# First attention of a two-block layer on one core: a head's first two groups of transposes leave the middle of the projection and join the short matmuls at the head's border

## What is computed

```python
q = rms_norm(q, q_norm_g) * (HEAD_DIM ** -0.5)
...
sc = jnp.einsum('brnikgh,brnjkh->brnkgij', ql, kb, preferred_element_type=jnp.float32)
...
sc = jnp.where(valid[:, None, None], sc + bias, -jnp.inf)
m = jnp.max(sc, axis=-1, keepdims=True)
p = jnp.exp(sc - m)
l = jnp.sum(p, axis=-1, keepdims=True)
o = jnp.einsum('brnkgij,brnjkh->brnikgh', p / l, vb.astype(jnp.float32))
...
alpha = jax.nn.softmax(jnp.stack(lses), axis=0)
o = jnp.sum(alpha[..., None] * jnp.stack(outs), axis=0).astype(x.dtype)
y = o.reshape(bsz, s, B_WIDTH) * jax.nn.silu(z)
```

## Time and profile before

| | us |
|---|---|
| median of 3 runs (lowest, highest) | 1373.73 (1373.12, 1374.71) |
| the profiled execution, its own time | 1375.31 |
| its span in the profile | 1373.5 |
| TensorE busy with matmuls (PE) | 1364.8 (99%) |
| TensorE's weight loads (PEld, beside PE) | 1169.5 (85%) |
| VectorE (DVE) busy | 1058.7 (77%) |
| ScalarE (ACT) busy | 718.5 (52%) |
| GpSimd (POOL) busy | 51.0 (4%) |

### The profile page before, as it was taken

One profiled execution on the slowest core, in us unless ns is written; L12 is line 12 of the kernel. 1 busy time (PEld: TensorE's weight loads), 2 busy tenths in 40 slices (PEclk: granted clock), 3 DMA queues, 4 the chain that ended last, 5 costly groups with the idle time before them and its releaser, 6 DMA issues.

```text
span 1373.5 us, 21419 instructions
## 1 busy us (share of the span) xinstructions
PE 1364.8 (99%) x7923; PEld 1169.5 (85%) x7923; DVE 1058.7 (77%) x1787; ACT 718.5 (52%) x1260; POOL 51.0 (4%) x55
## 2 busy tenths in 40 slices
PE   8999999999999999999999999999999999999999
PEld 6998888888889878888888787787688998998997
DVE  6976777777899788888888877778867965983883
ACT  4744333223357566666663566766646642662561
POOL 0000000000100000000001100000030000000000
PEclk9999999999999999999999999999999999999999
DMA  9994445457743211112212231111131232333232
GB/s 378 382 354 188 177 181 183 183 201 279 293 155 108 93 62 63 62 62 74 78 62 66 88 124 63 64 60 62 48 107 64 91 123 67 119 123 124 69 116 92
DMA packets 35350, 181.51 MB, mean 132 GB/s; under 512 B 4153, under 2 KB 4921, under 8 KB 20930
## 3 DMA queue, kind: packets, MB, share of 16 engines
q1 hardware_dynamic: 34050, 177.95, 35.7%
q10 hardware_dynamic: 1216, 2.44, 0.6%
HBM read 177.74 MB, written 2.11 MB: 131 GB/s over the span
## 4 chain that ended last, share of the span: by engine, by line
PE 97%; DVE 1%; ACT 1%; issue 0%; DMA 0%; DVEq 0%; ACTq 0%
PE acc L2121 72%; PE turn L2708 7%; PE ada L2121 4%; PE turn L2121 3%; PE norm L2121 3%; PE ada L2708 2%; PE acc L2708 2%; PE norm L2708 2%; PE turn L2565 1%; PE turn L2422 1%; DVE y_half L1209 0%; DVE w_lo L1217 0%; DVE wv_lo L1217 0%; ACT sq L697 0%; DVE k_t L1209 0%
## 5 line engine op out<-in xcount | busy, mean ns | idle before, releaser
L2121 PE MATMUL acc<-h_hi,w_hi 128*128 128x512 f32 x696 | 277.8, 399 | 0.0
L2121 PE MATMUL acc<-h_hi,w_lo 128*128 128x512 f32 x696 | 272.0, 391 | 0.0
L2121 PE MATMUL acc<-h_lo,w_hi 128*128 128x512 f32 x696 | 271.3, 390 | 0.0
L1217 DVE TENSOR_TENSOR w_lo<-w_raw,w_hi 128x2048 fp32r<-128x2048 f32 x58 | 136.4, 2352 | 27.7 <-ACT w_hi L680 27.7
L2121 PEld LDWEIGHTS acc<-h_hi,w_lo 128*128 128x128 f32 x696 | 130.6, 188 | 28.4
L2121 PEld LDWEIGHTS acc<-h_hi,w_hi 128*128 128x128 f32 x696 | 131.0, 188 | 27.1 <-issue 1.2
L2121 PEld LDWEIGHTS acc<-h_lo,w_hi 128*128 128x128 f32 x696 | 130.9, 188 | 25.6
L680 ACT ACTIVATE w_hi<-w_raw 128x2048 fp32r<-128x2048 f32 x60 | 114.3, 1906 | 29.4 <-PE acc L2121 28.6
L1209 DVE SCALAR_TENSOR_TENSOR x<-acc,mods,x 128x512 f32<-128x512 f32 x48 | 38.7, 813 | 68.6 <-PE acc L2121 68.6
L2121 PE MATMUL acc<-wv_hi,h_hi 128*128 128x256 f32 x320 | 90.5, 284 | 0.0
L2121 PE MATMUL acc<-wv_lo,h_hi 128*128 128x256 f32 x320 | 89.1, 279 | 0.0
(11 more groups left out here) (372 smaller groups left out, 3489.8 us busy)
## 6 DMA issues: line engine op xcount, KB each, us to landing
w_raw<-in_weights SPq DMA_DIRECT2D x102, 1024.0 KB, 4.9
ada_v<-in_ada SPq DMA_DIRECT2D x32, 512.0 KB, 6.3
ada_raw<-in_ada SPq DMA_DIRECT2D x32, 512.0 KB, 5.6
ada_out<-in_ada SPq DMA_DIRECT2D x32, 512.0 KB, 6.5
ada_up<-in_ada_first SPq DMA_DIRECT2D x8, 1024.0 KB, 16.3
w_raw<-in_weights SPq DMA_DIRECT2D x4, 768.0 KB, 4.3
x<-in_x SPq DMA_DIRECT2D x2, 1024.0 KB, 6.1
w_first<-in_weights SPq DMA_DIRECT2D x4, 512.0 KB, 13.3
```

The costliest lines, as they stand in the source:

```text
L1217: nc.vector.tensor_tensor(lo[:, 0:used], w_raw[par][:, 0:used], f32(hi[:, 0:used]), ALU.subtract).then_inc(lo_done, 1)
L2121: return nc.tensor.matmul(out, lhsT, rhs, start=start, stop=stop)
```

## The change

On TensorE, `turn(0)` and `turn(1)` no longer stand ahead of piece 3 in a projecting round. They open the next round instead, and the border gets a new order: transposes 0, 1 (of the head before), scores 0, 1, transposes 2, 3, values 0, 1, scores 2, 3, values 2, 3. In round 8, which doesn't project, transposes 0 and 1 of its own head stay about where they were. On ScalarE, `rstd_start(k + 2)` moves ahead of the copies of transposes 0 and 1, and the two passes of `z_start` ahead of the copies of 2 and 3. No instruction is added or removed, and SyncE's, GpSimd's and VectorE's queues are as they were.

```diff
--- before.py
+++ after.py
@@ -882,11 +882,12 @@
                     act.wait_ge(sum_done, k + mi)
                     square(G[mi % 2], sq_hi_q, sq[0])
 
+                if attend:
+                    z_start()
                 if mho is not None:
                     for c in (2, 3):
                         turn_copy(m - 1, c)
                 if attend:
-                    z_start()
                     exps(0)
                     exps(1)
                 if project:
@@ -908,11 +909,11 @@
                     rstd_start(k + 1, NB[:, :], P)
                     to_hi(u0 + 1, 0)
                     squares(2)
+                if project:
+                    rstd_start(k + 2, NB[:, :], P)
                 if attend:
                     for c in range(2 if project else 4):
                         turn_copy(m, c)
-                if project:
-                    rstd_start(k + 2, NB[:, :], P)
 
             def out_round(n, p, mho):
 
@@ -2414,23 +2415,25 @@
                     pe.wait_ge(apart_done, m + 1)
                     mm(T1[:, 0:64], spread, row_apart[:, :, :].rearrange("p c n -> p (c n)"), True, True).then_inc(spread_done, 1)
 
-                def turn(c):
-                    pe.wait_ge(p_ready, 4 * m + c + 1)
-                    if c >= 2:
-                        pe.wait_ge(pt_act, 4 * m + c - 1)
-                    for b, (tile, lo) in enumerate(TURNS[c]):
-                        turned = nc.tensor.transpose((T0, T1)[c % 2][:, P * b:P * b + P], s_b[tile][:, lo:lo + P], ident)
-                    turned.then_inc(turn_done, 1)
-
+                if prior:
+                    turn(m - 1, 0)
+                    turn(m - 1, 1)
                 if attend:
                     scores(0)
                     scores(1)
                 if prior:
-                    for c in (2, 3):
-                        values(m - 1, p, c)
+                    turn(m - 1, 2)
+                    turn(m - 1, 3)
+                    if not (isinstance(n, int) and n == 2):
+                        pe.wait_ge(head_out, m - 1)
+                    values(m - 1, p, 0)
+                    values(m - 1, p, 1)
                 if attend and prior:
                     scores(2)
                     scores(3)
+                if prior:
+                    values(m - 1, p, 2)
+                    values(m - 1, p, 3)
                 if project:
                     piece(0)
                 else:
@@ -2442,23 +2445,27 @@
                     piece(2)
                 else:
                     early_output(1, (0, 4, 1, 5), 6)
-                if attend:
-                    turn(0)
-                    turn(1)
                 if project:
                     piece(3)
                 else:
+                    turn(m, 0)
+                    turn(m, 1)
                     early_output(1, (2, 6), 6)
-                if attend:
-                    if prior:
-                        pe.wait_ge(head_out, m)
+                    pe.wait_ge(head_out, m)
                     values(m, q, 0)
                     values(m, q, 1)
-                    turn(2)
-                    turn(3)
-                if not project:
+                    turn(m, 2)
+                    turn(m, 3)
                     early_output(1, (3,), 7)
                     early_output(0, (3,), 7)
+
+            def turn(m, c):
+                pe.wait_ge(p_ready, 4 * m + c + 1)
+                if c >= 2:
+                    pe.wait_ge(pt_act, 4 * m + c - 1)
+                for b, (tile, lo) in enumerate(TURNS[c]):
+                    turned = nc.tensor.transpose((T0, T1)[c % 2][:, P * b:P * b + P], s_b[tile][:, lo:lo + P], ident)
+                turned.then_inc(turn_done, 1)
 
             def values(m, q, c):
```

## The result

| | kernel before | changed kernel |
|---|---|---|
| median of 6 runs each, same chip | 1373.14 us (1372.72 to 1374.71) | 1379.95 us (1378.16 to 1382.16) |
| ratio after to before | | 1.0049 [1.0038, 1.006] |
| profiled execution: time, span, granted clock | 1375.31, 1373.5, 1.00 | 1378.78, 1377.0, 1.00 |

The change makes the kernel 6.8 us slower (5.2 to 8.2 us by the interval). The forecast was 1378.9 us and slower, with a range of 1376.0 to 1381.2; the result lies in it.

What follows compares the result with a forecast made beforehand. TensorE, busy 1364.8 of 1373.5 us, was taken as the bound. Rounds 2 to 7 pay 4.20, round 1 1.08, round 8 gives back 0.11: 5.2 us slower, median 1378.9 us, whole range 1376.0 to 1381.2.

Steps and rivals of the forecast that it cites:

- first wait: TensorE waits for sq_lo_q at the sums inside piece 3, rounds 2 to 7: 0.31 plus 0.09, 0.40 us each.
- second wait: TensorE waits for VectorE's q_n at a border's first scores: 0.23 plus 0.09, 0.32 us in each of seven borders.
- moved group: Seven transposes moved from ahead of piece 3 to the border: 0.78 us saved, 0.76 paid, -0.02 a round; round 1 saves nothing.
- The first meeting: Sums inside piece 3 need sq_lo_q: TensorE there after 5.70 us, the other engines' chain allows 6.01.
- sums to sums: Time from norm<-sq_lo_q of piece 1 to norm<-sq_hi_q of piece 2: 6.48 us before, forecast 6.01.
- The second meeting: First scores need VectorE's last q_n pass: possible 3.96 us after piece 2's norm<-sq_lo_q, TensorE there at 3.73.
- 0.09 behind each wait: After a TensorE wait the next matmul stands 0.33 us behind instead of 0.24; charged at all 13 waits.
- rival (c): Further waits at scores 3, values 2 or the loop's register waits: 1.4 us more and up, 1380.3 to 1383; chance 0.10.
- 1.4 us kept for scores 3: Bound for a possible TensorE wait on VectorE's logits 1 at scores 3: 0.2 us in each of seven borders, none charged.
- (a): Rival: only one of the two waits comes, 1376.5 us with the second alone, 1376.7 with the first; chance 0.09.
- (b): Rival: not slower, ScalarE's passes run sooner and both chains end before TensorE arrives; 1374.3 us; chance 0.09.
- (d): Rival: TensorE's clock falls to 1.2 GHz in borders of 75 short matmuls; about 1437 us; chance 0.01.

Runs made afterwards that it cites:

- experiment 1: Changed kernel with ScalarE's squares of piece 2 ahead of its 1.90 us weight pass in rounds with attention; 1376.36 us, ratio 1.0022 to the kernel before.
- experiment 5: Kernel of experiment 1 with the sums of piece 2 ten matmuls into piece 3, not twelve; 1373.92 us, ratio 1.0009 to the kernel before.
- experiment 3: Kernel before with only the sums in piece 3 three matmuls earlier, transposes in their old place; 1376.12 us, ratio 1.0016.
- experiment 7: Changed kernel with the rounds loop written out on TensorE, ScalarE and VectorE, every wait against a constant; 1378.60 us, ratio 1.0043 to the kernel before.
- experiment 10: Changed kernel with ScalarE's z_start passes behind the copies of transposes 2 and 3 again; 1379.4 us in one run.
- experiment 8: The kernel before, unchanged, profiled a second time; 1373.42 us, span 1371.6.
- experiment 6: Kernel of experiment 5 with VectorE freeing piece 3's accumulator in round 1 ahead of the reciprocal's second half and z's gate; 1374.48 us, ratio 1.0009.
- experiment 4: Changed kernel with ScalarE's copies of transposes 0 and 1 ahead of rstd_start(k + 2) again; 1421.08 us in one run.

## Why the prediction was right

The runs split the 6.00 us. Taking the first wait away gives 226.96 - 224.18 = 2.78, the second too 224.18 - 221.70 = 2.48, and 0.74 is left (experiments 1 and 5).

| term | predicted | measured |
|---|---|---|
| first wait, rounds 2 to 7 | 6 x 0.40 = 2.40 | 2.78 |
| second wait, borders 1 to 7 | 7 x 0.32 = 2.24 | 2.48 |
| moved group: 6 x -0.02, 0.76 in border 1, -0.11 in round 8 | 0.53 | 0.74 |
| sum in the rounds | 5.17 | 6.00 |

- **Moving the group.** With no waits, rounds are as long as before to within the 0.03 us that they scatter by; over distances 2 to 6 of experiment 5 that is 0.03 more in all, where five times -0.02 would be -0.10. So the move is free, as forecast, and its small gain is not seen. In round 1's border the group was to cost 0.76; the first distance of experiment 5 has 0.81.
- **The first meeting.** Shown. TensorE by itself would be there after 5.70 us (5.69 in experiment 1), sums to sums is the forecast 6.01 in the rounds outside the loop, and experiment 3 shows the same end with the transposes in their old place.
- **The second meeting.** Shown: 3.96 us in every border that is outside the loop. The 0.09 behind each wait held too, 0.33 against 0.24; that the late weight load makes it is argued, and no run tested it. The Trainium skill (TensorE: Matmul & The Clock Gate, Step-by-step: what each phase is for) says that weight loads are pulled ahead of matmuls in flight. The step speaks of no load behind an unmet wait, and at such a place the trace shows none pulled ahead: the load at 578.71 begins with its matmul, and the 1.2 us less that the prediction worked out from the rule did not come.
- **The mis-sized term.** The forecast took both waits as long in the loop as in rounds 0 and 1, and priced the alternative only under rival (c). In the loop the first takes 0.07 us more in rounds 3 to 6 and the second 0.085 in four borders: 0.62 us of the 0.83 that are missing, and experiment 7 gives back 0.61. With it the two waits come to 4.64 + 0.62 = 5.26, which is 2.78 + 2.48 as measured. The other 0.21 lie in the third row: by the distances of experiment 5 round 1 pays 0.81 for 0.76, distances 2 to 6 together 0.03 for -0.10, and the last -0.10 for -0.13. They have no cause shown.
- **Round 1** pays 1.14 (1.08), and its idle place is as described. **Round 8's** 0.11 came, 0.34 to 0.24, but not for the reason given. The prediction had TensorE come later against the others; experiment 10 leaves TensorE as late and has the wait back. The gain belongs to `z_start`'s new place, so that term was right by luck.
- **What was taken as free** was free: copies, scores 3, `z_start` in rounds 1 to 7 (experiment 10). The 1.4 us kept for scores 3 were not needed, though its slack was only 588.07 - 587.93 = 0.14 us by the rows of the border. Of the rivals, (a) falls, since both waits are there; (b) falls, since neither chain got shorter (5.95 and 3.89 us, where rows 4 and 6 have 5.95 and 3.90); of (c) only the loop's waits came, at 0.62 us; (d) falls at waits of this size.
- **Two slips in the sum's bounds.** 13 waits 0.1 us shorter give 1378.9 - 1.3 = 1377.6, not 1377.4, and the bound of scores 3 gives 1380.3, not 1380.4. Neither touches the forecast.
- **The sum against the clock.** The medians differ by 6.8 us [5.2, 8.2] and the rounds by 6.00. Runs of one kernel lie up to 5 us apart (1375.07 to 1380.13 in experiment 1), and experiment 8 finds 2 us of such spread in a stage that the change doesn't touch; the 0.8 between the two numbers is no more than that. The forecast of the loss was 5.2 us and 6.8 were measured, 1.6 more: 0.83 in the rounds, the rest in this spread. That the time came within 1.05 us of 1378.9 is in part luck, since the forecast starts from 1373.73 and the six runs have 1373.14.

No version beats the kernel before: the best, experiment 5, is level with it in rounds 2 to 7 and 0.74 us behind in all.

## What to carry to other kernels

The seven short transposes between long matmuls cost TensorE next to nothing more than among other short ones (0.02 us by the rows, and not to be seen in the runs), so merging them gained nothing here; what the move changes is the time at which TensorE arrives everywhere else. Before work is moved on the bounding engine, list each meeting with another engine between the old place and the new, write its slack (here 6.48 - 6.01 = 0.47 us where 0.78 was taken, and 5.40 - 3.96 = 1.44 where 1.67 was) and move only what fits. If it doesn't, shorten the chain first on the helping engine, as experiments 1 and 5 do, and look again at the meeting behind it, as experiment 6 didn't.

## What the runs showed of the hardware

- At a wait that TensorE has to stand out it starts 0.05 to 0.06 us after the end of VectorE's record outside the loop and 0.13 to 0.15 inside it, where the awaited count depends on the loop's variable (578.65 to 578.70 in experiment 7, 578.58 to 578.72 in the changed kernel). A wait that is met already shows no such difference: in the kernel before, sums to sums is 6.48 to 6.49 and the scores stand 5.40 to 5.41 behind the sums in rounds 2 to 7, in the loop and outside it.
- The weight load of a matmul that waits begins with it, at 578.71 and 578.72 in the changed kernel, and the next matmul stands 0.33 behind where 0.24 is usual.
- Behind 4.09 to 4.26 us of idle time at each of the seven borders of experiment 4 TensorE ran at 0.50 of its clock, 1.2 GHz. Beyond the wait that cost 1.5 to 1.7 us in five borders and 2.8 to 2.9 in two. The idle time of 1.50 us in experiment 6 had no such stretch behind it: the granted clock is 1.00 from 514.1 to 520 us, and from the second distance on its matmuls stand 0.22 to 0.24 apart.
- The first stage ran at 0.117 us a matmul of 256 columns in one execution of the kernel before and at 0.113 in another, at a granted clock of 1.00 in both and with less from the DMA engines in the slower (353 and 368 GB/s). What decides it was not tried.
